# A gated feed-forward on one core: the hidden blocks of the first output group are split four products later

## The reference, cut to what matters

```
def conv_ffn(x, w_in, conv_w, conv_b, w_out):
    h = causal_depthwise_conv(x @ w_in, conv_w, conv_b)
    val, gate = jnp.split(h, 2, axis=-1)
    return (jax.nn.silu(gate) * val) @ w_out
x = x + conv_ffn(rms_norm(x, norm_ffn_g), w_in, conv_w, conv_b, w_out)
```

## Time and profile before

| | |
|---|---|
| time, median of 3 runs | 2355.59 us (2355.25 to 2358.07) |
| the profiled execution | 2354.93 us, span 2353.1 us |
| mean granted clock of TensorE | 0.993 |
| products 0 to 181 | 1868.1 us to 2350.0 us of the span |

### The profile page before, as it was taken

One profiled execution on the slowest core, in us unless ns is written; L12 is line 12 of the kernel. 1 busy time (PEld: TensorE's weight loads), 2 busy tenths in 40 slices (PEclk: granted clock), 3 DMA queues, 4 the chain that ended last, 5 costly groups with the idle time before them and its releaser, 6 DMA issues. The chain is left out here.

```text
span 2353.1 us, 35362 instructions
## 1 busy us (share of the span) xinstructions
PE 2271.7 (97%) x11778; PEld 1934.2 (82%) x11778; DVE 1598.8 (68%) x3281; ACT 1310.6 (56%) x3022; POOL 683.0 (29%) x843
## 2 busy tenths in 40 slices
PE   7999999999999999999999999898999999999999
PEld 6888888888888878888888888787777888887887
DVE  7444677677885343346666566669788778889787
ACT  6454566666775444456665556655556645455542
POOL 3454332311145642222222222555563200000000
PEclk9999999999999999999999999999999999999999
DMA  7322101111243342222223233523343633345734
GB/s 228 118 72 68 40 25 32 35 36 49 65 137 98 96 130 72 86 75 90 83 91 95 71 94 95 190 86 110 93 139 111 196 96 94 117 143 170 232 113 139
DMA packets 332355, 241.68 MB, mean 103 GB/s; under 512 B 66448, under 2 KB 284816, under 8 KB 331664
## 3 DMA queue, kind: packets, MB, share of 16 engines
q1 hardware_dynamic: 332176, 239.43, 33.6%
HBM read 195.59 MB, written 43.78 MB: 102 GB/s over the span
## 5 line engine op out<-in xcount | busy, mean ns | idle before, releaser
L2835 POOL TENSOR_TENSOR WS<-WR,WS 128x256 fp32r<-128x256 f32 x635 | 493.2, 797 | 1005.3 <-ACT WS L2176 1004.4
L1935 PE MATMUL PS<-HT,WS 128*128 128x512 f32 x1492 | 602.7, 404 | 20.2 <-POOL WS L2835 5.8
L1937 PE MATMUL PS<-HT,WS 128*128 128x512 f32 x1492 | 585.1, 392 | 0.0
L1936 PE MATMUL PS<-HT,WS 128*128 128x512 f32 x1492 | 582.9, 391 | 0.0
L1935 PEld LDWEIGHTS PS<-HT,WS 128*128 128x128 f32 x1492 | 281.4, 189 | 78.2 <-issue 13.4
L1937 PEld LDWEIGHTS PS<-HT,WS 128*128 128x128 f32 x1492 | 280.8, 188 | 61.1
L1936 PEld LDWEIGHTS PS<-HT,WS 128*128 128x128 f32 x1492 | 281.9, 189 | 51.8
L2176 ACT ACTIVATE PT<-PS 128x512 fp32r<-128x512 f32 x352 | 185.9, 528 | 198.9 <-PE PS L2048 198.4
L2176 ACT ACTIVATE WS<-WR 128x256 fp32r<-128x256 f32 x658 | 245.3, 410 | 81.9 <-PE PS L1937 55.2
L2424 DVE TENSOR_TENSOR PT<-PS,PT 128x512 fp32r<-128x512 f32 x352 | 211.1, 609 | 84.7 <-ACT PT L2176 81.8
L2081 PE MATMUL PS<-PT,QKV 128*128 128x256 f32 (+1 forms) x1248 | 208.4, 289 | 3.2 <-DVE YB L2603 2.4
(11 more groups left out here) (282 smaller groups left out, 4585.4 us busy)
## 6 DMA issues: line engine op xcount, KB each, us to landing
WR<-in_w_in_odd SPq DMA_DIRECT2D x106, 256.0 KB, 2.9
EO<-in_grid SPq DMA_DIRECT2D x48, 384.0 KB, 3.1
WR<-in_ffn_in SPq DMA_DIRECT2D x60, 256.0 KB, 3.0
WR<-in_w_in_even SPq DMA_DIRECT2D x100, 128.0 KB, 2.5
WR<-in_w_out_odd SPq DMA_DIRECT2D x48, 256.0 KB, 2.9
yd<-PY SPq DMA_DIRECT2D x44, 256.0 KB, 3.3
EO<-in_ffn_in SPq DMA_DIRECT2D x35, 256.0 KB, 3.1
WR<-in_w_in_even SPq DMA_DIRECT2D x34, 256.0 KB, 2.9
```

The lines of the kernel that those rows point to most:

```text
L1935: e.matmul(out, wh, rh, start=start, stop=False)
L1936: e.matmul(out, wh, rl, start=False, stop=False)
L1937: return e.matmul(out, wl, rh, start=False, stop=stop)
L2835: e.tensor_tensor(ws(i, 1, n), RAW[raw_slot(u)][:, o:o + n], f32(ws(i, 0, n)), ALU.subtract).then_inc(s_wlop.sem, 1)
```

## The change

The hidden blocks of group 0 are split at steps 90 to 103 where they were split at steps 86 to 99. Groups 1 and 2 keep their steps. Nothing is added or removed; the products, which engine does what, and the condition under which a block may be overwritten (the last argument, `s0 - 14 + 2 * b + 2`) stay.

```
--- before.py
+++ after.py
@@ -1811,7 +1811,7 @@
                     fetch_hidden()
                 for s0, g in start.items():
                     for z in range(4):
-                        b, z2 = divmod(t - (s0 - 14) - 2, 2)
+                        b, z2 = divmod(t - (s0 - 14) - (6 if g == 0 else 2), 2)
                         if 0 <= b < 7 and z // 2 == z2 and z < GROUPS[g][1]:
                             split_hidden(g, b, z, s0 - 14 + 2 * b + 2)
                 if t == 14 * entered + 10:
```

## The result

| | before | changed |
|---|---|---|
| median of 14 runs each | 2357.40 us (2355.25 to 2359.89) | 2362.07 us (2359.57 to 2367.73) |
| ratio, 95% interval | | 1.0022 (1.0014 to 1.0030) |
| profiled execution, span | 2354.93 us, 2353.1 us | 2360.77 us, 2359.0 us |
| product 0 to product 110 | 304.78 us | 308.53 us |

The changed kernel is slower by 0.22%, some 5 us. In the two profiled executions the stretch from product 0 to 110 took 3.75 us more. The rest of their difference of 5.9 us in span lies ahead of product 0, in work that the change doesn't touch: product 0 starts at 1870.20 instead of 1868.10.

The account below looks back on a forecast made before the run. VectorE's total work, not TensorE's pace, was taken to set the stretch's end. The 4.5 us won at 96 is given back at 110; the new wait adds 3.6: 2358.5 profiled, 2359.2 us median (+0.15%), range 2355.0 to 2361.3.

Parts of the forecast that it names:

- The wait at 96: At product 96: post 92 starts 4.8 us earlier, so the 2.79 wait and the clock's 1.69 go, 4.5 us.
- VectorE does not run dry in steps 87 to 92: In the lightened steps, tightest at step 90, VectorE still does not wait, by 0.1 us; lost: 0.
- The gain is given back at 110: All 28 low halves still precede post 106, so product 110 starts at 2172.9 again; 4.5 us given back, sum 0.
- The new wait: ScalarE's posts of 98 and 99 wait for VectorE's low halves of b = 4; VectorE then loses 3.6 us.
- The three terms, 1.25, 1.05 and 1.25: VectorE's waits for ScalarE: weights of step 99, high half of b = 4's third block, weights of step 100.
- Product 110 at +3.6: Post 106 starts at 2175.5, so product 110 starts at 2176.5 instead of 2172.88, +3.6 us.
- the covered fall of the clock: If the clock falls at product 106 after 3 us idle, its 1.7 us is covered by the wait at product 110.
- the 2 to 3 that I listed as a sign: TensorE's idle time at product 110 in the changed trace, expected to be 2 to 3 us.
- a load of b = 6: Later loads may delay ScalarE by 1 or 2 us; cost 0, up to 1. Rival: over 2 us, chance 0.04.
- The time: Whole kernel: profiled 2354.93 plus 3.6 gives 2358.5; median 0.66 above the profiled one, so 2359.2 us, +0.15%.
- the rival with 0.24: Idle 3 us before 106 does not lower the clock; it falls uncovered around 110: +5.3, 2360.9 us; chance 0.24.
- 0.66 to within it: Chance 0.66 that the measured time stays within 0.2% (4.7 us) of the kernel before.

Follow-up runs that it names:

- half the shift: Against the changed kernel, hidden blocks of group 0 split two products later instead of four; product 0 to 110 took 304.75 us, ratio 0.9998 against the kernel before.
- other rooms: Against the changed kernel, rooms handed out in another order so b = 3, not b = 4, lies in X4 and X6; 304.77 us to product 110, ratio 0.9997.
- b = 4 alone: Against the kernel before, only the four blocks of b = 4 split four products later; 310.39 us to product 110, ratio 1.0022.
- sums later: Other rooms, plus four sums of hidden blocks moved from steps 104 and 105 to 107 and 108; 303.23 us to product 110, ratio 0.9995.

## Why the prediction was right and where it was wrong

*The wait at 96* went with its fall of the clock, and post 92 started 4.8 earlier (2128.45, which is 2126.35 when the 2.10 us by which product 0 came later are taken off; 2126.4 was forecast). Right.

*VectorE does not run dry in steps 87 to 92.* Right: it waited nowhere between step 86 and step 99.

*The gain is given back at 110.* Right, and shown three times: half the shift and other rooms reach product 110 where the kernel before did, and VectorE with seven low halves fewer moves it by 3.66 of their 4.2 us.

*The new wait.* Right in place and kind. The three terms, 1.25, 1.05 and 1.25, were reckoned from the moment when VectorE's next row could have started. So reckoned, which adds to each idle time the 0.09 by which two rows overlap, the trace has 1.35, 1.05 and 1.35, in sum 3.75 for 3.6; the post of 106 started 3.76 later. Other rooms shows that they vanish when other blocks lie in X4 and X6.

*Product 110 at +3.6.* Measured +3.75 in two executions; the waits before it at 102, 103 and 106 (2.99 idle, 3 forecast) and the covered fall of the clock were as described. The idle time at 110 itself was 1.37, not the 2 to 3 that I listed as a sign: that list left out the 1.7 that the fall at 106 takes from it, which the sum had as covered. ScalarE did wait for a load of b = 6, for 0.2 us.

*The time.* 2362.07 lies outside the range, whose upper end was 2361.3. The step that failed is the one from the stretch to the time: "The median is 0.66 above the profiled one, so I forecast 2359.2 us". It took the level of the kernel before from three runs. Fourteen gave 2357.40, 1.8 higher, and later sets of 33, 27 and 21 runs gave 2357.89, 2357.05 and 2357.67. The profile I had was itself the earliest: over ten other profiled executions product 0 started between 1868.66 and 1877.09, against 1868.10. With the right level the same step gives 2361.0. The range held terms for the mechanism and none for this. Of the 2.9 us between forecast and measured median, the level is 1.8 and the stretch 0.15; the other 0.9 stays open.

*What is left.* The medians differ by 4.7, the ratio says 5.2 (3.3 to 7.1) and, repeated, 3.1 (0.9 to 5.2), where the stretch has 3.75. All these overlap. That in some executions the clock falls where nothing covers it, the rival with 0.24, was seen in neither profiled execution of the changed kernel; whether it adds to its median stays open. So does on which side of 0.2% the kernel truly lies; I gave 0.66 to within it and 0.30 to slower. Of the reasons that I gave for that rival, a wait "longer than the 2.63 that lowered it before" is a weak one: in b = 4 alone the clock stayed up behind 2.62 and 2.81 us.

## What to carry to other kernels

If an engine is busy without a break between two points, a wait that one of its posts causes inside that stretch is not a place to win: moving rows from before the wait to behind it moves the wait, as long as the end of the stretch waits for that engine too. Win by taking work out of the stretch, behind the last post that is waited for, as silu, gating and sums were here. And when a producer is moved later, look at who writes over its source: a buffer that serves as a landing room and as an output tile ties the two engines together, and how many steps lie between them is the cushion.

## What the hardware showed that I had not expected

GpSimd's subtraction of 128x512 took 1.29 us at its shortest and 4.51 at its longest, and cost VectorE 1.07 us on average, more than the 0.60 that it took over. And how long TensorE had been idle did not tell whether its clock would fall to 1.2 GHz. It fell behind idle times of 2.63 us (before, at product 96), 2.99 (changed, at 106), 2.19 (other rooms, at 106) and 2.15 (sums later, at 106), while behind half the shift's 2.03 at the same product it stayed up. But in b = 4 alone it stayed up behind 2.62 at product 96 and 2.81 at 102, where the matmuls behind the first kept taking 0.39 to 0.40, and fell at 103, behind 2.31.
